# Two transformer blocks in one program: second block's layers written out, gates of the scatter on GpSimd, constant products at stage borders

## The reference

```python
def reference(...):
    x = first_block(x, c, ctx, c_ctx, ...)      # attention + pooling + Fourier branches, conv FFN, two streams
    return second_block(x, ...)

def second_block(x, ...):
    for l in range(DEPTH):
        xn = rms_norm_2(x, norm1_g[l])
        x = x + mixing_sublayer(xn, ...)         # 16 heads of three kinds, then w_out
        xn = rms_norm_2(x, norm2_g[l])
        x = x + peer_ffn(xn, ...)
    return x

def peer_ffn(xn, wq, sub_keys, u_tab, v_tab):    # t = 256 tokens, 8 heads, 16384 experts
    q = jnp.matmul(xt, wq).reshape(t, PEER_HEADS, 2, PEER_SUBDIM)
    scores = jnp.einsum('thcd,hcnd->thcn', q, sub_keys)
    sv, si = lax.top_k(scores, PEER_TOPK)
    ...
    best_s, best_p = lax.top_k(cand_s, PEER_TOPK)
    idx = jnp.take_along_axis(cand_i, best_p, axis=-1)
    gate = jax.nn.softmax(best_s, axis=-1)
    ...
        act = jnp.einsum('td,thkd->thk', xb, u_tab[ib])
        wgt = jax.nn.gelu(act) * gb
        return jnp.einsum('thk,thkd->td', wgt, v_tab[ib])
```

## Time and profile before

| | |
|---|---|
| Time, median of 3 runs | 3555.29 us (3544.3, 3555.29, 8444.94) |
| The profiled execution | 3550.49 us, its span 3548.6 us |
| Mean granted clock | 0.963 |
| PE busy | 3318.6 us (94%) |
| DVE busy | 2463.7 us (69%) |
| ACT busy | 1801.6 us (51%) |
| POOL busy | 389.7 us (11%) |
| DMA | 510.96 MB, mean 144 GB/s |

### The profile page before, as it was taken

One profiled execution on the slowest core, in us unless ns is written; L12 is line 12 of the kernel. 1 busy time (PEld: TensorE's weight loads), 2 busy tenths in 40 slices (PEclk: granted clock), 3 DMA queues, 4 the chain that ended last, 5 costly groups with the idle time before them and its releaser, 6 DMA issues. The chain is left out here.

```text
span 3548.6 us, 65522 instructions
## 1 busy us (share of the span) xinstructions
PE 3318.6 (94%) x20396; PEld 2896.1 (82%) x20396; DVE 2463.7 (69%) x4979; ACT 1801.6 (51%) x3483; POOL 389.7 (11%) x300
## 2 busy tenths in 40 slices
PE   7889999999889998999789999998999779999999
PEld 6757776778669998789668999997889768999998
DVE  5567776767565775569876777776659877777776
ACT  4443343333356655646764444444646764444454
POOL 0000000000000001548100000000648200000000
PEclk7899999999899998999999999999999999999999
DMA  5115433434215454335036666665335136656665
GB/s 187 54 66 178 163 125 134 142 119 154 72 60 170 159 175 150 109 124 173 12 124 185 188 186 186 188 185 168 122 116 167 35 96 189 186 186 188 185 188 166
DMA packets 139372, 510.96 MB, mean 144 GB/s; under 512 B 15984, under 2 KB 16368, under 8 KB 138224
## 3 DMA queue, kind: packets, MB, share of 16 engines
q1 hardware_dynamic: 138528, 506.65, 44.6%
q10 hardware_dynamic: 720, 2.71, 0.2%
HBM read 508.25 MB, written 1.05 MB: 144 GB/s over the span
## 5 line engine op out<-in xcount | busy, mean ns | idle before, releaser
L266 ACT ACTIVATE split<-ring 128x512 fp32r<-128x512 f32 (+1 forms) x1700 | 1061.5, 628 | 1425.3 <-PE ps L204 1351.5
L273 DVE TENSOR_TENSOR split<-ring,split 128x512 fp32r<-128x512 f32 (+1 forms) x1404 | 956.9, 686 | 662.3 <-ACT split L266 639.7
L204 PE MATMUL ps<-h2T,split 128*128 128x256 f32 x7776 | 987.3, 285 | 10.2 <-DVE h2T L507 8.8
L204 PEld LDWEIGHTS ps<-h2T,split 128*128 128x128 f32 x7776 | 971.1, 193 | 30.8 <-DVE h2T L507 11.1
L204 PE MATMUL ps<-split,chunk 128*128 128x512 f32 x3072 | 739.6, 393 | 18.2 <-DVE chunk L2484 16.2
L204 PEld LDWEIGHTS ps<-split,chunk 128*128 128x128 f32 x3072 | 567.0, 189 | 129.8 <-DVE chunk L2484 16.6
L204 PE MATMUL ps<-hT,split 128*128 128x512 f32 (+1 forms) x3504 | 641.7, 344 | 15.9 <-DVE hT L509 8.8
L273 POOL TENSOR_TENSOR split<-ring,split 128x512 fp32r<-128x512 f32 x296 | 389.5, 1332 | 2384.3 <-ACT split L266 2378.5
L204 PEld LDWEIGHTS ps<-hT,split 128*128 128x128 f32 x3504 | 544.6, 191 | 109.3 <-DVE hT L509 13.2
L204 PE MATMUL ps<-act_chunk,split 128*128 128x512 f32 (+1 forms) x1056 | 188.3, 339 | 13.6 <-DVE act_chunk L619 13.6
L2351 PE MATMUL ps<-ring 128*128 128x128 f32 x1024 | 151.0, 293 | 49.8 <-DVE ring L2329 49.4
(11 more groups left out here) (345 smaller groups left out, 3010.3 us busy)
## 6 DMA issues: line engine op xcount, KB each, us to landing
ring<-peer_uv SPq DMA_DIRECT2D x456, 512.0 KB, 3.5
ring<-w_up SPq DMA_DIRECT2D x88, 512.0 KB, 3.4
ring<-w_choose SPq DMA_DIRECT2D x88, 512.0 KB, 3.6
ring<-w_mixing SPq DMA_DIRECT2D x72, 512.0 KB, 3.6
ring<-w_merge SPq DMA_DIRECT2D x64, 512.0 KB, 3.4
ring<-w_down SPq DMA_DIRECT2D x44, 512.0 KB, 3.3
mix_row_ring<-w_mod SPq DMA_DIRECT2D x40, 512.0 KB, 3.7
ffn_row_ring<-w_mod SPq DMA_DIRECT2D x40, 512.0 KB, 3.6
```

Of the source, the lines that this page charges most:

```text
L204: ins = nc.tensor.matmul(out, lhsT(a), rhs(b), start=first and n == 0, stop=last and n == len(PASSES) - 1)
L266: self.nc.scalar.activation(self.split[:, s % SPLIT, 0, cols], self.ring[:, s, cols], ACT.Copy).then_inc(self.high_ready, 1)
L273: (ops or self.nc.vector).tensor_tensor(self.split[:, s % SPLIT, 1, cols], self.ring[:, s, cols], self.split[:, s % SPLIT, 0, cols].bitcas ...
```

## The change

- **Loop to Python.** The loop over the two layers of the second block is written out. The last layer has no norm to sum for and no mixing tiles to load ahead. `stage` loses its argument `again`, with which four semaphores were cleared one by one on GpSimd at the end of the mixing stage.
- **Memset.** In the mixing stage DVE clears `k.blank` behind the norm's lead.
- **Output.** In the last layer SP stores each pair of chunks of `x2T` (256 KB) as soon as it is added.
- **Scatter.** The iota is copied to PSUM once a stage, and DVE's comparisons read it there. DVE makes `hot_i` for all four tokens and `hot_j` for three; ACT makes the fourth `hot_j` as relu(1 - |slot - iota|) in two steps, the second waiting for the first; GpSimd multiplies the four `hot_i` by their gates in one step.
- **Constant products.** `hold_clock` issues fp32 products of the identity with the 384 columns of `const_sb` into a PSUM bank that nothing reads then. In the diff's order they stand in a lead behind the root's spread (2), at the start of `residual_stage` (4), at the end of `qk_stage` (4), at the start of `natural_stage` (1), at the ends of `merge_stage` and `ffn_up_stage` (4 each), in `choose_stage` ahead of the transposes (3), at the end of `scatter_stage` (2) and at the start of `experts_stage` (7).

```diff
+def hold_clock(k, bank, n):
+    for _ in range(n):
+        k.nc.tensor.matmul(k.ps[:, bank, 0:CONST_W], k.const("ident"), k.const_sb[:, :], start=True, stop=True)
...
         self.spread_root(pe)
+        hold_clock(self.k, 7, 2)
         for c in range(DC):
             pe.wait_ge(self.h_low, (c + 1) * self.streams)
...
             weights.slots_free(pe)
+            hold_clock(k, 7, 4)
...
             swap(n - 1)
+            hold_clock(k, 7, 4)
...
             weights.slots_free(pe)
+            hold_clock(k, 6, 1)
...
             turns(pe, n_tiles, use, unrolled=rows is not None)
+            hold_clock(k, 7, 4)
...
             turns(pe, n_tiles, use, unrolled, SPLIT)
+            hold_clock(k, 7, 4)
...
-            nc.vector.memset(k.blank.bitcast(U32), 0).then_inc(blanked, 1)
             dve.wait_ge(gains_in, 16)
             norm1.lead_dve(dve, weights)
+            nc.vector.memset(k.blank.bitcast(U32), 0).then_inc(blanked, 1)
             dve.wait_ge(loads_in, 16 * len(loads))
...
+            pe.wait_ge(scores_used, HC + RAW)
+            hold_clock(k, 7, 3)
             pe.wait_ge(kept, n_tiles + RAW)
...
-    iota = k.const("iota").unsqueeze(1).broadcast_to([P, lot, NK])
+    on_act = 1
+    iota_psum = k.ps[:, lots, 0:NK]
+    iota = iota_psum.unsqueeze(1).broadcast_to([P, lot, NK])
...
             def one_hots(i, n):
                 dve.wait_ge(spread, i * lots + n + 1)
-                for hot, slot, many in ((k.hot_i, k.slot_i, lot - 1), (k.hot_j, k.slot_j, lot)):
...
+                for hot, slot, first in ((k.hot_i, k.slot_i, 0), (k.hot_j, k.slot_j, on_act)):
...
-                nc.vector.tensor_scalar(k.hot_i[:, n * lot + lot - 1, :], k.const("iota"), k.slot_i[:, t], k.slot_gate[:, t],
-                                        ALU.is_equal, ALU.mult).then_inc(one_hot, 1)
...
+        @block.gpsimd
+        def _(pool):
+            with pool.Fori(0, turns_all) as i:
+                for n in range(lots):
+                    pool.wait_ge(one_hot, (i * lots + n) * 2 + 1)
+                    hot = k.hot_i[:, n * lot:(n + 1) * lot, :]
+                    gates = k.slot_gate[:, bass.ds(token(i, n), lot)].unsqueeze(2).broadcast_to([P, lot, NK])
+                    nc.gpsimd.tensor_tensor(hot, hot, gates, ALU.mult).then_inc(gated, 1)
...
                     pe.wait_ge(weighted, i * lots + n + 1)
-                    pe.wait_ge(one_hot, (i * lots + n) * 3 + 3)
+                    pe.wait_ge(one_hot, (i * lots + n) * 2 + 2)
+                    pe.wait_ge(act_hot, i * lots + n + 1)
+                    pe.wait_ge(gated, i * lots + n + 1)
...
+            hold_clock(k, 7, 2)
...
-            def gate(i, n):
-                act.wait_ge(one_hot, (i * lots + n) * 3 + 1)
-                for u in range(lot - 1):
-                    hot = k.hot_i[:, n * lot + u, :]
-                    nc.scalar.activation(hot, hot, ACT.Copy,
-                                         scale=k.slot_gate[:, bass.ds(token(i, n) + u, 1)]).then_inc(gated, 1)
+            def one_hots(i, n):
+                act.wait_ge(spread, i * lots + n + 1)
+                hot = k.hot_j[:, n * lot, :]
+                nc.scalar.activation(hot, k.const("iota"), ACT.Abs, scale=-1.0,
+                                     bias=k.slot_j[:, bass.ds(token(i, n), 1)]).then_inc(distance, 1)
+                act.wait_ge(distance, i * lots + n + 1)
+                nc.scalar.activation(hot, hot, ACT.Relu, scale=-1.0, bias=1.0).then_inc(act_hot, 1)
...
+            if not norm:
+                for m in range(pairs):
+                    sp.wait_ge(added, m + 1)
+                    sp.dma_start(out_dram[:, 2 * m:2 * m + 2, :], k.x2T[:, 2 * m:2 * m + 2, :]).then_inc(stored, 16)
+                sp.wait_ge(stored, 16 * pairs)
...
             weights.slots_free(pe)
+            hold_clock(k, 7, 7)
...
-    with nc.Fori(0, DEPTH) as l:
+    for l in range(DEPTH):
...
-        with stage(nc, "stored") as (block, stored):
...
-                sp.dma_start(out, k.x2T[:, :, :]).then_inc(stored, 16)
```

More of the change, by code:

```diff
@@ L107, in stage @@
 @contextmanager
-def stage(nc, *names, weights=None, again=False):
+def stage(nc, *names, weights=None):
     sems, every = [], list(weights.loaded) if weights else []
@@ L2316, in lagged @@
             keep(turns_all - 1, n)
-    with stage(nc, "one_hot", "gated", "spread", "copied", "weighted") as (block, one_hot, gated, spread, copied, weighted):
+    with stage(nc, "one_hot", "gated", "spread", "copied", "weighted", "iota_kept", "distance", "act_hot") as (
+            block, one_hot, gated, spread, copied, weighted, iota_kept, distance, act_hot):
         @block.vector
@@ L2368, in keep, with experts_stage @@
                     k.ps[:, n, :].rearrange("p (t j) -> p t j", t=lot)[:, :, EARLY:NK], ACT.Copy).then_inc(copied, 1)
-            lagged(act, gate, keep, 1)
-def experts_stage(k, weights, norm, ahead):
+            lagged(act, one_hots, keep, 1)
+def experts_stage(k, weights, norm, ahead, out_dram):
     nc, n_tiles = k.nc, EARLY + 2 * (NK - EARLY)
@@ L2400, in prepare_ahead @@
             prepare(i + (s + SPLIT) // RAW, (s + SPLIT) % RAW)
-    with stage(nc, *WEIGHT_SEMS, "gelu_done", "weight_step", "weighted", "kept_0", "kept_1", "turned", "added", *Norm.SUMS, weights=weights) as (
-            block, high_ready, low_ready, halves_used, gelu_done, weight_step, weighted, kept_0, kept_1, turned, added, squared, sums_done):
+    with stage(nc, *WEIGHT_SEMS, "gelu_done", "weight_step", "weighted", "kept_0", "kept_1", "turned", "added", "stored", *Norm.SUMS, weights=weights) as (
+            block, high_ready, low_ready, halves_used, gelu_done, weight_step, weighted, kept_0, kept_1, turned, added, stored, squared, sums_done):
         weights.signals(high_ready, low_ready, halves_used)
-        norm.sum_signals(squared, sums_done)
+        if norm:
+            norm.sum_signals(squared, sums_done)
         @block.sync
@@ L2448, in _ @@
                 ins.then_inc(turned, 1)
-            norm.add_up(pe)
+            if norm:
+                norm.add_up(pe)
         @block.scalar
@@ L2469, in _ @@
                 nc.scalar.activation(k.y_natural[:, 0, half * 512:(half + 1) * 512], outs[half], ACT.Copy).then_inc(kept_0, 1)
-            norm.warm(act)
-            for m in range(pairs):
+            if norm:
+                norm.warm(act)
+            for m in range(pairs if norm else 0):
                 act.wait_ge(added, m + 1)
@@ L2705, in program @@
         with ExitStack() as scope:
-            second_block(k, scope, sb)
-        with stage(nc, "stored") as (block, stored):
-            @block.sync
-            def _(sp):
-                sp.dma_start(out, k.x2T[:, :, :]).then_inc(stored, 16)
-                for loaded in k.mixing.loaded:
-                    sp.wait_ge(loaded, 16)
-                sp.wait_ge(stored, 16)
+            second_block(k, scope, sb, out)
 def packed(table, width, parts):
```

26 lines of the change are left out of this document (11 added, 15 removed).

## The result

Eight runs of each kernel: the median before is 3550.6 us, of the changed kernel 3517.2 us. The ratio of the changed kernel's time to that of before is 0.9913, with a 95% interval of 0.9897 to 0.9928: 31 us faster by the ratio (33 by the medians), which lies within 2%. The forecast was 3510. The profiled execution of the changed kernel took 3523.8 us (span 3522.0), 6.6 above its median, and that of before 3550.5. Span against span the trace has 26.6 us to account for.

A forecast was written before the change was run, and what follows sets the result against it. TensorE was taken to bound most of the program, VectorE the two scatter stages, and waits the borders. Scatter 13.6, constant products 15.4, layers and memset 4.0 and output 7.0 summed to 40.0 off 3550.5: 3510 us, range 3484 to 3536.

The forecast's parts named there:

- Scatter, 13.6 forecast: Two scatter stages of 64 lots: 16.6 us gained by a faster lot, less 3 for filling, iota copy and constant products.
- GpSimd then sets the pace: 1.38 against 1.51: Scatter: GpSimd's one instruction of 512 elements a lot bounds the lot at 1.38 us, where it took 1.51.
- the loop through the engines: Scatter: hot, GpSimd, PE, ScalarE's copy, hand-over and weighing take 4.0 us over three lots, 1.33 each, below GpSimd's 1.38.
- slower by contention: Rival, chance 0.05: GpSimd at its slowest or DVE's steps doubled in scatter, 2.45 us a lot, 3647 us in all.
- Constant products, 15.4 forecast: Stage borders and norm leads: products filling PE's waits keep the clock up, 10.7 plus 4.7 us, bounds -5 and +34.
- the first group: Eight half-clock stretches after borders, 35.6 us of PE time, 17.8 to gain at best; six tenths taken, 10.7 us.
- delay PE by 2 to 3: Borders behind merge or ffn_up: at half clock four products take 6 us and delay PE, cancelling what the clock gives back.
- a quarter: Norm leads: of eight low-clock stretches holding 37.9 us of PE time, part comes back by two products each, 4.7 us.
- Layers written out and memset, 4.0 forecast: Second block's mixing stage entries: 3.4 us gained in the second layer and 0.6 in the first.
- DVE waits there for 2.1 us, so its 1.98 us are covered: Mixing stage, between lead and gate step: the moved memset costs nothing; without cover, 2 us a layer.
- Constant products buy nothing: Rival, chance 0.18: the clock falls anyway or PE starts later; term -5 to 3, time 3523 to 3530 us.
- Scatter stays at 1.51: Rival, chance 0.13: GpSimd's register-computed addresses or broadcast gates cost 0.13 more a lot; time 3527 us.

The follow-up runs named there:

- Experiment 3: The changed kernel, but DVE's comparisons in scatter read the iota from SBUF and no copy to PSUM is made: 3580.8 us, ratio 1.0095 to the kernel before.
- experiment 4: The changed kernel without any constant product: 3538.1 us, ratio 0.9963 to the kernel before.
- experiment 5: The changed kernel with the scatter of the kernel before and without any constant product: 3539.6 us, ratio 0.9967 to the kernel before.
- experiment 9: The changed kernel with weighing three lots behind and k.blank cleared by GpSimd, without constant products in the leads only: 3503.5 us, ratio 0.9861 to the kernel before.

## Why the prediction was right, and where it wasn't

**The time** came out 7 us above the forecast, inside the range and in its "within 2%". By the medians 33 us of the 40 are there, in the profiled pair 26.6; that the medians come out nearer is no merit of the forecast, since the eight runs of the changed kernel lie between 3510.3 and 3537.9. It was a sum of which one term was far too large, one too large, and two held. One reading was off by one: behind the first slice the clock row has three eights, not four; no term uses it.

**Scatter, 13.6 forecast, 5.3 measured.** The step that failed is "GpSimd then sets the pace: 1.38 against 1.51". Both halves were off. GpSimd's multiplication takes 1.04, not the 1.30 of the subtraction in the earlier trace rows; the price came from the nearest row of another operation and operand. And the loop through the engines, which I had named and set at 4.0 us or 1.33 a lot, takes 4.17 to 4.55. Of the 4.17, the steps up to the next `hot_i` are 0.68 + 1.04 + 1.13 + 0.50 + 0.22 = 3.57, and four hand-overs make 0.60 where I had put 0.2; at other places of a turn it is up to 0.4 more. With my 1.30 for GpSimd the same loop would have come out above 1.45. The right loop was written down and then dropped because a mis-sized number stood above it. The losses around it were about right: filling the pipe takes 4.9 to 5.0 us instead of 3.9 (0.5 and 0.3 to 0.4 forecast).

**Contention.** The reading of the earlier trace rows held: with the iota in PSUM the step of 512 stayed at 0.69. Experiment 3 shows the price of the opposite: 1.91 a lot, which is past the 1.69 from which the kernel is slower than before. The rival "slower by contention" was one operand away.

**Constant products, 15.4 forecast, 13.1 in the trace, 14 to 18 by experiment 4.** The right size, of another make. At the borders nearly all of the first group came back, since the dips of the earlier trace rows are gone but for parts of two. The step "delay PE by 2 to 3" at half clock didn't happen there: with four products ahead of the barrier the clock is still at 1.00 behind merge, and behind ffn_up in layer 0, where it does fall, the delay is 0.7. In the leads "a quarter" (4.7) was too low: the five with 256 tokens gave 8.0.

**Layers written out and memset, 4.0 forecast, 1.4 measured.** The second entry gained 4.35 (forecast 3.4, bounds to 3.9) and the first 0.8 (0.6), but 1.3 and 2.5 of it went again behind the two leads. What failed is "DVE waits there for 2.1 us, so its 1.98 us are covered". That wait was for PE at half clock. The same change brings the clock back, PE is through the lead's 48 products at 1397.8 and waits 2.28 and 2.72 us for the gate step, together 5.0 where it was 1.5. Without the products the wait goes with the clock of the lead as well: 0.74 to 0.84 us in three leads at 0.58 to 0.61, and 2.10 in the one that ran at 0.71 (experiments 4 and 5). I had named the price without cover, 2 us a layer, but not that another part of this change takes the cover away.

**Output, 7.0 forecast, 6.8 measured.** The last store was estimated at 2.2 and landed in 2.4 us.

**The rivals.** "Constant products buy nothing" fell with experiments 4 and 9. "Scatter stays at 1.51" was as far from the truth in that stage as the forecast's 1.38 (1.43 and 1.47; 5.3 us between -3 and 13.6), and what slows the lots is not what it names, GpSimd's addresses.

## What to carry over

When several engines hand a buffer round in a ring, price the loop first, with a measured hand-over (0.13 to 0.19 us each here) for every arrow, and compare it with every engine's own pace; one more lot of lag was worth 20.4 us where the moved work had brought 5.3. A cover that consists of another engine being slow vanishes when the same change makes it fast. A filler belongs only where its last instruction ends before the signal that is waited for.

## What the runs showed of the hardware

- A DVE step with both inputs in SBUF ended only 0.55 us after GpSimd's instruction (1.34 us for 0.69); with one input in PSUM it kept its 0.69 beside it.
- GpSimd multiplies 128 x 512 by a gate broadcast along the keys in 1.04 us, and subtracts two full tiles of that size in 1.27 to 1.30 (minimum and median).
- The same instructions at the same place ran 14 us at 0.53 or at 1.00 of the clock, which made 12 us between two executions. The attention and pooling stages of layer 0 differed by up to 12 us in the same way. Effects under that were read from the stages, not from the medians.
